# Forget logits in paired columns, moved pieces of matmuls and copies, and another order of loads, splits and banks in the feed forward part

## The reference

```python
h = rms_norm(x); proj = h @ w_in     # rq rk rv rg | fq fk fv fl | cb cc ch
A = group_norm(retention(rotary(rq), rotary(rk), rv)) * silu(rg)       # 4 heads of 64
logf = log_sigmoid(fl + bias)                                         # 8 forget logits a token
B = forgetting_attention(norm(fq), norm(fk), fv, cumsum(logf))         # 8 heads of 64
C = cb * causal_conv3(cc * ch)                                        # 256 channels
x = x + concat(A, B, C) @ w_out
h2 = rms_norm(x)
x = x + (silu(causal_conv3(h2 @ w_gate)) * (h2 @ w_up)) @ w_down       # 2816 wide
```

## Time and profile before

| what | value |
|---|---|
| median of 3 runs | 1673.87 us (1672.96 to 1674.76) |
| the profiled execution, whole | 1675.11 us |
| its span, first to last instruction | 1673.1 us |
| PE busy | 1616.4 us, 97% |
| DVE, ACT, POOL busy | 1109.9, 681.6, 391.4 us |
| a turn of the feed forward loop, 10 in each layer | 38.9 us |
| mean granted TensorE clock | 0.995 |
| DMA | 160.8 MB, mean 96 GB/s |

### The profile page before, as it was taken

One profiled execution on the slowest core, in us unless ns is written; L12 is line 12 of the kernel. 1 busy time (PEld: TensorE's weight loads), 2 busy tenths in 40 slices (PEclk: granted clock), 3 DMA queues, 4 the chain that ended last, 5 costly groups with the idle time before them and its releaser, 6 DMA issues.

```text
span 1673.1 us, 29200 instructions
## 1 busy us (share of the span) xinstructions
PE 1616.4 (97%) x10278; PEld 1395.4 (83%) x10278; DVE 1109.9 (66%) x1760; ACT 681.6 (41%) x1273; POOL 391.4 (23%) x520
## 2 busy tenths in 40 slices
PE   7999998899999999999999999999999999999998
PEld 5758896678899999999887688866888999999997
DVE  4336446537987778888644463565298888888884
ACT  4213336414544444444332133463164444444442
POOL 1103200103433333333112040000044333333330
PEclk9999999999999999999999999999999999999999
DMA  8204421831222222222242233237222222222221
GB/s 248 75 12 109 139 89 68 279 108 51 88 85 79 75 75 79 84 90 81 73 117 63 66 79 127 85 113 270 76 64 76 75 88 87 89 87 75 75 75 68
DMA packets 125028, 160.80 MB, mean 96 GB/s; under 512 B 25604, under 2 KB 77262, under 8 KB 124622
## 3 DMA queue, kind: packets, MB, share of 16 engines
q1 hardware_dynamic: 124808, 159.44, 29.9%
q10 hardware_dynamic: 144, 0.33, 0.1%
HBM read 150.22 MB, written 9.53 MB: 95 GB/s over the span
## 4 chain that ended last, share of the span: by engine, by line
PE 75%; DVE 13%; issue 5%; DVEq 3%; ACT 2%; ACTq 1%; DMA 1%; SPq 0%; POOL 0%; POOLq 0%
PE bank L2037 70%; PE bank L2099 5%; DVE x L1865 3%; DVE wlo L1422 3%; DVE gact L1895 2%; ACTq L1362 1%; DVEq L1977 1%; DMA raw<-in_w_in 1%; DVE h L1884 1%; DVEq L1761 0%; DVE wlo L1408 0%; ACT pf L1243 0%; DVE hlo L1432 0%; DVE h L1912 0%; DVE pf L1764 0%
## 5 line engine op out<-in xcount | busy, mean ns | idle before, releaser
L2037 PE MATMUL bank<-whi,hhi 128*128 128x512 f32 x560 | 226.1, 404 | 2.7 <-DVE hlo L1432 1.6
L2037 PE MATMUL bank<-whi,hlo 128*128 128x512 f32 x560 | 220.2, 393 | 0.0
L2037 PE MATMUL bank<-wlo,hhi 128*128 128x512 f32 x560 | 219.9, 393 | 0.0
L2037 PE MATMUL bank<-hhi,whi 128*128 128x320 f32 (+1 forms) x672 | 210.4, 313 | 1.0 <-DVE hlo L1432 1.0
L2037 PE MATMUL bank<-hlo,whi 128*128 128x320 f32 (+1 forms) x672 | 209.0, 311 | 0.0
L2037 PE MATMUL bank<-hhi,wlo 128*128 128x320 f32 (+1 forms) x672 | 208.8, 311 | 0.0
L1408 DVE TENSOR_TENSOR wlo<-raw,whi 128x1024 fp32r<-128x1024 f32 (+1 forms) x84 | 98.8, 1181 | 124.1 <-ACT whi L1050 122.9
L2037 PE MATMUL bank<-whi,guhi 128*128 128x512 f32 x440 | 176.0, 400 | 3.2 <-DVE gulo L1432 2.0
L2037 PE MATMUL bank<-whi,gulo 128*128 128x512 f32 x440 | 173.6, 395 | 0.0
L2037 PE MATMUL bank<-wlo,guhi 128*128 128x512 f32 x440 | 173.5, 394 | 0.0
L1865 DVE TENSOR_TENSOR x<-x,bank 128x512 f32<-128x512 f32 x220 | 139.0, 680 | 21.6 <-PE bank L2037 21.3
(11 more groups left out here) (285 smaller groups left out, 3640.7 us busy)
## 6 DMA issues: line engine op xcount, KB each, us to landing
raw<-in_w_in SPq DMA_DIRECT2D x52, 512.0 KB, 3.6
raw<-in_w_gate SPq DMA_DIRECT2D x44, 512.0 KB, 3.7
raw<-in_w_down SPq DMA_DIRECT2D x44, 512.0 KB, 3.6
vb<-in_cache_fox_v SPq DMA_DIRECT2D x16, 1024.0 KB, 7.5
raw<-in_w_up SPq DMA_DIRECT2D x24, 512.0 KB, 3.5
gains<-in_w_up SPq DMA_DIRECT2D x20, 512.0 KB, 3.5
raw<-in_w_out SPq DMA_DIRECT2D x16, 512.0 KB, 4.8
kb<-in_cache_fox_k SPq DMA_DIRECT2D x8, 1024.0 KB, 7.0
```

Of the source, the lines that this page charges most:

```text
L2037: return pe.matmul(out, lhsT=lhsT, rhs=rhs, start=start, stop=stop, skip_group_check=True)
```

## The change

- Forget logits: high and low weights lie side by side in a home of their own (`wfl`), so two matmuls of 16 columns (high and low part of h) take the place of three of 8; the two halves of the result are summed in `flT`, which becomes a product with a 0/1 matrix (`fsum`).
- Retention: of the five pieces ahead of units 2 to 6 that of unit 4 goes ahead of unit 1; the one after `rst` goes ahead of `rds0`.
- Convolution's copies: ACT's copy of `hhi[6:8]` is one unit later, DVE's low part behind the maxima and scales of n=6.
- Second norm: the splits of gate slabs 1 and 2 go one tile later, behind tiles 3 and 4.
- Homes: `w_up`'s first slab gets a home of its own, `raw_up0`, where `t2f` lay; `t2f` lies on the place of `t3l`, with one drain more on DVE. Slot 2 of `raw` is loaded once a turn and no longer twice, and the order of SP's loads changes.
- The loop: `down_hi(0)` stands after the copy of `a1`, `down_hi(1)` after that of `a2`, `down_lo(0)` at the head of the turn.
- Last rows and end: other banks for the last rows and for `down_end`; the last `gu` is split in two halves, with DVE's splits of the last down slabs ahead of the multiplication of `a4`.

```diff
+    put("fsum", (p[:, None] < 2 * FH) & (p[:, None] % FH == np.arange(FH)[None, :]))
...
+LAST_BANKS = (0, 1, 2, 4, 5, 6)
+END_BANKS = (3, 7, 0, 1, 2, 4, 5, 6, 3, 7)
...
+    return [(("d", "end", nc, t), END_BANKS[2 * t + nc]) for t in range(TT) for nc in range(2)]
...
+        j(("last", g), LAST_BANKS[g])
...
-            [("t2f", [P, 4, HALF], F32)],
+            [("raw_up0", [P, 1024], F32)],
...
-        eb = own("eb", [P, 2, P], F32R)
+        (eb, wfl) = region([("eb", [P, 2, P], F32R)], [("wfl", [P, KT, 2, FH], F32R)])
...
+            src = raw[:, s, :] if kind == "g" else gains[:, :] if j == 1 else raw_up0[:, :]
...
-        PER_TURN = (1, 2, 2)
+        PER_TURN = (1, 2, 1)
...
+
+            k = 4 * (n - FL)
+            return wfl[:, k:k + 4, lo_, :]
...
                 def ffn_loads(it, further):
-                    for j, e in ((3, 4), (4, 6)):
-                        load(LOOP0 + j, l, ffn_src(j, it), (e, it))
-                    for j, e in ((2, 7), (0, 8), (1, 13)) if further else ():
+                    load(LOOP0 + 3, l, ffn_src(3, it), (4, it))
+                    for j, e in ((1, 6), (2, 7), (0, 8)) if further else ():
                         load(LOOP0 + j, l, ffn_src(j, it + 1), (e, it))
                     if further:
+                        wait_lo(sp, 13, l, it)
+                        apart(sp)
+                        load_up(0, it + 1)
                         wait_lo(sp, 15, l, it)
                         apart(sp)
-                        load_up1(it + 1)
-
-                def load_up1(it):
-                    src = ffn_src(5, it)
-                    sp.dma_start(gains[:, :].rearrange("p (k n) -> p k n", k=src.shape[1]), src).then_inc(up1_in, 16)
-
-                for j in range(3):
-                    load(LOOP0 + j, l, ffn_src(j, 0))
+                        load_up(1, it + 1)
+
+                def load_up(i, it):
+                    src = ffn_src(4 + i, it)
+                    dst = (raw_up0, gains)[i]
+                    sp.dma_start(dst[:, :].rearrange("p (k n) -> p k n", k=src.shape[1]), src).then_inc(up_in[i], 16)
+
+                load(LOOP0, l, ffn_src(0, 0))
+                load(LOOP0 + 1, l, ffn_src(1, 0))
+                load_up(0, 0)
                 sp.wait_ge(xn_ready, l * (2 * TT) + 2 * TT)
                 apart(sp)
-                load_up1(0)
+                load_up(1, 0)
+                load(LOOP0 + 2, l, ffn_src(2, 0))
                 with sp.Fori(0, PAIRS - 2) as it:
                     ffn_loads(it, True)
                 ffn_loads(PAIRS - 2, False)
-                for c, e in ((0, 8), (1, 13)):
...
                 wait_loaded(act, n, l)
+                if n in (FL, FL + 1):
+                    act.activation(forget_part(n, 0), forget_raw(n), ACT.Copy).then_inc(hi_split, 1)
...
                             ins.then_inc(B.free[B.bank(key)], 1)
-                        if n == 4:
+                        if n == 5:
                             B.wait_taken(act, ("cb_", 1, 1), l)
                             act.activation(hhi[:, 6:8, :], oc[:, :, :], ACT.Copy).then_inc(cat_hi, 1)
...
-                norm(1, l, {0: G0, 2: G0 + 1, 3: G0 + 2})
+                norm(1, l, {0: G0, 3: G0 + 1, 4: G0 + 2})
...
                     part_hi("g", i, l, 0)
-                B.wait_full(act, ("u", "pro", 1, 1), l)
-                down_hi(0, l, 0)
...
                     act.wait_ge(gu_done, it + (l * PAIRS + 1))
                     act.activation(guhi[:, :, :], gu[:, :, :], ACT.Copy).then_inc(gu_hi, 1)
                     copied("g", "c1", it)
-                    B.wait_full(act, ("g", "loop", "c1"), l, it)
+                    copied("g", "a2", it)
                     down_hi(1, l, it)
-                    copied("g", "a2", it)
                     for i in range(4):
                         up_hi(i, l, it)
...
                     else:
+                        B.wait_full(act, ("d", "loop", 1, TT - 1), l, it)
+                        split(DLAST, l)
                         copied("u", "a1", it)
                         copied("u", "c1", it)
-                        B.wait_full(act, ("u", "loop", "a2"), l, it)
-                        split(DLAST, l)
+                        split(DLAST + 1, l)
                         copied("u", "a2", it)
-                        B.wait_full(act, ("u", "loop", "a3"), l, it)
-                        split(DLAST + 1, l)
                 with act.Fori(0, PAIRS - 2) as it:
                     pair(it, True)
                 pair(PAIRS - 2, False)
+                act.wait_ge(gu_first, l + 1)
+                act.activation(guhi[:, 0, :], gu[:, 0, :], ACT.Copy).then_inc(gu_hi_end, 1)
                 act.wait_ge(gu_done, l * PAIRS + PAIRS)
-                act.activation(guhi[:, :, :], gu[:, :, :], ACT.Copy).then_inc(gu_hi, 1)
+                act.activation(guhi[:, 1, :], gu[:, 1, :], ACT.Copy).then_inc(gu_hi_end, 1)
...
                     if n < NU:
                         fox_max(n)
                     if n < NU + 1:
                         fox_scale(n - 1)
+                    if n == 6:
+                        dve.wait_ge(cat_hi, l * HIS + 1)
+                        lo(hlo[:, 6:8, :], oc[:, :, :], hhi[:, 6:8, :]).then_inc(cat_lo, 1)
...
-                norm(1, l, {0: G0, 2: G0 + 1, 3: G0 + 2}, completed)
+                norm(1, l, {0: G0, 3: G0 + 1, 4: G0 + 2}, completed)
...
+                dve.drain()
                 t_low(3)
...
...
-                    dve.wait_ge(gu_hi, it + (l * PAIRS + 1))
+                    down_lo(0, l, it)
+                    dve.wait_ge(gu_hi, it + (l * (PAIRS - 1) + 1))
...
                     gate_lo(6)
                     key = ("u", "loop", "a4")
                     B.wait_full(dve, key, l, it)
                     dve.tensor_tensor(gu[:, 1, 0:HALF], bank[B.bank(key)][:, 0:HALF], gact[:, 1, 0:HALF],
...
-                        split(DLAST, l)
-                        split(DLAST + 1, l)
                 with dve.Fori(0, PAIRS - 2) as it:
                     pair(it, True)
                 pair(PAIRS - 2, False)
-                dve.wait_ge(gu_hi, l * PAIRS + PAIRS)
-                lo(gulo[:, :, :], gu[:, :, :], guhi[:, :, :]).then_inc(gu_ready, 1)
+                for ft in range(2):
+                    dve.wait_ge(gu_hi_end, l * 2 + ft + 1)
+                    ins = lo(gulo[:, ft, :], gu[:, ft, :], guhi[:, ft, :])
+                ins.then_inc(gu_ready, 1)
                 if l + 1 == DEPTH:
                     for t in range(TT):
...
                     ready(FL + i, l)
-                    s_ = slot(FL + i)
-                    for half in range(2):
-                        key = ("fl", half)
-                        if i == 0:
-                            B.wait_room(pe, key, l)
-                        for k in range(4):
-                            ws = slice(k * FH, k * FH + FH)
-                            ts = slice(half * HALF, half * HALF + HALF)
-                            ins = mm3(bank[B.bank(key)][0:FH, 0:HALF], whi[:, s_, ws], wlo[:, s_, ws], hhi[:, 4 * i + k, ts],
-                                      hlo[:, 4 * i + k, ts], i == 0 and k == 0, i == 1 and k == 3)
-                        if i == 1:
-                            fill(ins, key)
-                    if i == 0:
-                        ins.then_inc(slab_used, 1)
+                for half in range(2):
+                    key = ("fl", half)
+                    B.wait_room(pe, key, l)
+                    ts = slice(half * HALF, half * HALF + HALF)
+                    for k in range(KT):
+                        for h_ in (hhi, hlo):
+                            ins = mm(bank[B.bank(key)][0:2 * FH, 0:HALF], wfl[:, k, :, :].rearrange("p s n -> p (s n)"),
+                                     h_[:, k, ts], k == 0 and h_ is hhi, k == KT - 1 and h_ is hlo)
+                        if half == 1 and k == 3:
+                            ins.then_inc(slab_used, 1)
+                    fill(ins, key)
                 chunk(1, l, "rt", lambda t: pe.wait_ge(rot_ready, l * TT + t + 1))
                 for half in range(2):
...
-                transposes("flT", [(bank[B.bank("flT")][:, t * FH:(t + 1) * FH], flr[:, t * P:(t + 1) * P])
-                                   for t in range(TT)], l)
+                B.wait_room(pe, "flT", l)
+                for t in range(TT):
+                    ins = mm(bank[B.bank("flT")][:, t * FH:(t + 1) * FH], flr[:, t * P:(t + 1) * P], K("fsum")[0:2 * FH, :], True, True)
+                fill(ins, "flT")
...
-                    if 2 <= n <= 6:
+                    if n in (1, 2, 3, 5, 6):
...
-                piece(l)
...
-                    if h == 2:
+                    if h % 2 == 0:
```

More of the change, by code:

```diff
@@ L273, in end_jobs @@
 def end_jobs():
-    return [(("d", "end", nc, t), 3 + (2 * t + nc) % 5) for t in range(TT) for nc in range(2)]
+    return [(("d", "end", nc, t), END_BANKS[2 * t + nc]) for t in range(TT) for nc in range(2)]
 def plan_banks(banks):
```

(6 more changed lines are left out.)

38 lines of the change are left out of this document (20 added, 18 removed).

## The result

The changed kernel takes 1676.24 us (median of 20 runs, 1674.79 to 1678.18), the kernel before in the same comparison 1674.01 (20 runs, 1672.42 to 1676.95). The ratio is 1.0015, 95% interval 1.0008 to 1.0021: slower by 0.15%, where 1670.0 and a gain was forecast. The step is small, and clear of noise. The profiled execution took 1675.17, and its span is as long as that of before.

What follows compares the result with a forecast made beforehand. PE was taken as the bound, busy 1616.4 us of a span of 1673.1. Terms 2 x (-2.25 - 1.4 - 2.35 + 3.1 + 0.1) + 1.9 = -3.7 gave a median of 1670.0, range 1663.0 to 1676.0.

Steps and rivals of the forecast that it cites:

- Forget logits, retention, copies: Fewer forget matmuls, filled retention gaps, shorter PE wait for scaled probabilities: -2.25, -1.4 and -2.35 us a layer.
- Norm and homes at the entry: First feed forward turn: longer DVE chain and POOL's earlier w_up sums beside DVE's low parts delay `a4`: +3.1 us a layer.
- the 6 that I worked out from it: Entry: by the exclusion rule alone four POOL sums could hold DVE for 6 us, in place of 2.1 to 3.
- Later turns: Feed forward loop after the first turn: 0 us a turn, bounds -0.06 and +0.5.
- The collision that I feared, in the up products: Later turns: POOL's last w_up sum meets DVE's multiplications of `gu`, which is done 1.3 to 1.7 us later.
- End of a layer: Ahead of the down product: same DVE work and one instruction more, +0.1 us a layer, bounds -1 and +0.5.
- The boundary: Layer 1's first matmul waits for bank 3, which the last tile takes: +1.9 us once, bounds 0 and +2.
- an upper bound of the entry: First turn: +4.5 us a layer, if a gap of 3 brings 1.2 GHz, 1.2 more.
- The rival that ended slower, a loop that slips by the late `guhi`: Feed forward loop: PE's `a4` product waits in each turn; with a loss of 0.45 it is 1679; chance 0.14.

Runs made afterwards that it cites:

- end_bank_7: Changed kernel with banks 7 and 4, not 3 and 7, for the last tile of the last down product: 1672.57 us, ratio to before 0.9985.
- end_splits: Changed kernel with DVE's splits of the last two down slabs in its pauses between the last up products' adds: 1670.22 us, ratio to before 0.9972.
- loads_ahead: Changed kernel with POOL's waits for the loaded gate weights ahead of its wait for the taps: 1670.08 us, ratio to before 0.9978.
- sums_ahead: Changed kernel with POOL's sums of the next gate weights ahead of the saving of the last rows: 1683.71 us, ratio to before 1.0055.
- change_mended: Changed kernel with its homes, POOL's waits ahead, DVE's last splits in its pauses, and banks 7 and 4 for the last tile: 1660.55 us, ratio 0.9910.
- homes_only: Kernel before with only the homes and the order of loads and down splits of the change: 1681.55 us, ratio 1.0035.
- pool_held: Changed kernel with POOL's first-turn pads and w_up sums held until DVE's last low part of the prologue's gate weights: 1677.6 us, ratio to before 1.0020.
- last_banks: Kernel before with six different banks for the last rows and 3, 7, 0, 1, 2, 4, 5, 6, 7, 4 for the last down product: 1677.31 us, ratio 1.0010.

## Why the prediction was wrong

By its own steps, layer 0 and layer 1:

- **Forget logits, retention, copies**: -6.0 in each forecast, -6.95 and -5.53 measured. The places are right, and two sizes (the forget logits 4.70 for 4.68; the waits of 0.85 and 0.60 are gone). The copies were put too high: the waits for scaled probabilities fell from 2.78 + 0.20 to 0.20 + 0.20 + 0.99, by 1.6 and not 2.35. That layer 0 gained 1.4 more than layer 1 is luck: there the trace of before has one stretch more at a low granted clock, behind the wait for `rso` (0.54 from 121.0 to 124.5), which the changed kernel's trace has not. Other traces of these edits have it: of the 20 such stretches in the ten kernels with these edits, 6 take 235.2 and not 233.6.
- **Norm and homes at the entry**: +3.1 forecast, +2.98 and +2.91 measured, through the chain described. Counted from the norm, DVE's three parts begin 2.0 later and take 2.5 longer, the copy of `gu` comes 4.5 later, `a3` 3.5, `a4` 3.0. The mechanism is right; that the number is so close is partly luck. Six kernels have this same entry (the changed one, `end_bank_7`, `end_splits`, `loads_ahead`, `sums_ahead`, `change_mended`); 5 of their 12 entries take 59.9 to 60.1, the other 7 take 60.9 to 61.0, with a second stretch at a low granted clock in the first turn. The profiled execution has the short kind twice. The Trainium skill ("SBUF — State Buffer", "Who interferes with whom") lets the loser wait for the whole instruction. The rows agree as to who waits: the parts, which read SBUF twice, and not the multiplications, which read a bank. They don't bear out the 6 that I worked out from it: the three parts of `homes_only` take 4.4 where they took 1.9, so the sums held DVE for 2.5.
- **Later turns**: 0 forecast; +0.06 a turn measured, 1.1 in 18 turns. The collision that I feared, in the up products, cost nothing, as worked out. What I missed stands at the other end of the turn: an instruction more in POOL's queue ahead of the gate sums. I had compared the order of its sums, not the waits between.
- **End of a layer**: +0.1 forecast, +0.22 measured by the start of the down product. The step that failed is behind it. I counted the merged pause of 2.38 by its length and not by what follows it. With a low granted clock layer 1's down product took 1.5 more, and layer 0's 1.6 more than the 18.7 of `pool_held` and `sums_ahead`, where the same two pauses stand and the clock stayed at full.
- **The boundary**: +1.9 forecast, 2.0 measured; and behind it 1.6 more at a low clock.

The failed step is therefore one in the main: **I took a new pause of PE at its length.** The terms of the end and of the boundary, +0.1 and +1.9, have nothing for the clock. I had put its price, 1.2, into an upper bound of the entry, but into no other term, though the earlier trace rows showed it behind a pause of 2.35. It is 4.7 us in the profile: 1.6 + 1.5 + 1.6. With 1.1 for the turns, which I had put at 0, this makes the forecast of -3.7 into +2.1; measured are +1.7 in the traces and +2.2 by the medians. The rival that ended slower, a loop that slips by the late `guhi`, was not what happened.

How far each part of the 4.7 belongs to the new pauses, this count of all traces shows:

| place | pauses of PE ahead of it | clock fell behind them |
|---|---|---|
| last down product, layer 0 | 0.91 and 0.98 (old end) | 3 of 5 |
| the same | 2.10 (`last_banks`) | 1 of 1 |
| the same | 2.38 (new end) | 3 of 5 |
| the same | 0.20 (splits moved) | 0 of 3 |
| last down product, layer 1 | 0.91 and 0.98 | 0 of 5 |
| the same | 2.10 | 0 of 1 |
| the same | 2.38 | 4 of 5 |
| the same | 0.20 | 0 of 3 |
| layer 1's first matmul | 1.76 | 2 of 5 |
| the same | none | 0 of 9 |

So layer 1's 1.5 goes with the new pause, and the boundary's 1.6 came only where the pause stood, though not each time. Layer 0's 1.6 isn't shown to: there the old end had a low clock as often, and the profiled execution of before was one of those without.

## What to carry to other kernels

Where PE is the bound, look at new pauses twice: for their length and for the granted clock behind them, and price both from rows at either level. The second price is a chance: read it from several traces, not from one. Where two engines exclude each other, the start of one short instruction decides, and an instruction of a queue that waits for nothing still delays what stands behind it: put waits that are long fulfilled ahead of the one that comes last. Before moving a transfer earlier, ask which work it releases and what that will lie beside; here the new home removed POOL's wait of 17 us, which had cost nothing, and what POOL then did earlier held DVE.

## What the runs showed of the hardware

How often the clock falls behind a pause goes with its length here, and not with that alone. At the last down product, a place with the same work in all kernels, the profiled executions show a low granted clock in 7 of 10 cases behind a pause of 2.38, in 3 of 10 behind two of 0.91 and 0.98, in 1 of 2 behind one of 2.10 and in 0 of 6 behind one of 0.20; but the 3 of 10 are all in layer 0, where the 2.38 does no worse (table above). Behind the 1.76 at the boundary it fell in 2 of 5. Which case comes isn't fixed by the program: it costs 1.5 to 1.6 us each time at these places, and 0.9 in the first turn. In every kernel the slower runs tend to be those with the lower mean clock (before: 0.996 in the run of 1672.68 us, 0.994 in that of 1677.82), so several such places probably make up most of what lies between the fastest and the slowest run of one kernel, 3.4 us for the changed one.

Removing 0.34 us of an idle engine's queue gave 6 us in all: POOL's sum starts earlier, so DVE's low part is held for less, so the bank is free in time, in 18 turns.
